# Picking expert numbers on VectorE: 16-bit pairs and lists in SBUF, and a tree of four additions in place of a reduction

## The reference

```
q = (h @ w_query).reshape(tokens, 8 heads, 256)
s1, s2 = scores of the two halves of q against 128 keys each
v1, i1 = top_k(s1, 16);  v2, i2 = top_k(s2, 16)
cand = (v1[:, None] + v2[None, :]).reshape(256)
top_s, top_c = top_k(cand, 16)
e1 = i1[top_c // 16];  e2 = i2[top_c % 16]
expert = e1 * 128 + e2
g = softmax(top_s)
act = gelu(u_tab[expert] . h);  out = sum(g * act * v_tab[expert])
```

## Time and profile before

| | us |
|---|---|
| median of 3 runs | 1533.51 |
| runs | 1533.39 to 1535.49 |
| span of the profiled execution, first to last instruction | 1527.6 |
| the profiled execution's own time | not listed; the median less the span is 5.9 |
| PE busy in the span | 1499.3 (98%) |
| DVE busy | 1196.7 (78%) |
| POOL busy | 1018.7 (67%) |
| ACT busy | 703.2 (46%) |

### The profile page before, as it was taken

The page is one execution under the profiler, slowest core; times in us unless marked ns, Lnnn a source line. Parts: engine busy times, 40 slices in busy tenths (PEclk is TensorE's granted clock), DMA queues, the critical chain, the costliest instruction groups (busy, mean ns, idle before and its releaser), DMA issues.

```text
span 1527.6 us, 21847 instructions
## 1 busy us (share of the span) xinstructions
PE 1499.3 (98%) x7983; PEld 1254.4 (82%) x7983; DVE 1196.7 (78%) x1979; ACT 703.2 (46%) x1312; POOL 1018.7 (67%) x623
## 2 busy tenths in 40 slices
PE   8999999999999999999999999999999999999997
PEld 4336684488899999999999999988888887888886
DVE  6858833526799899998888880288998898899998
ACT  2024653343344433488888883433333333333333
POOL 2602002653378888776777875698888888889866
PEclk8999999999999999999999999999999999999999
DMA  9976138033178898889999997799999999999981
GB/s 365 337 222 114 29 99 287 37 129 110 39 268 320 318 329 309 295 295 374 362 374 365 378 358 296 261 371 360 379 373 363 376 388 379 373 384 377 374 282 69
DMA packets 216600, 439.99 MB, mean 288 GB/s; under 512 B 38181, under 2 KB 128805, under 8 KB 214573
## 3 DMA queue, kind: packets, MB, share of 16 engines
q1 hardware_dynamic: 178764, 303.49, 56.7%
q0 software_dynamic: 36864, 134.23, 23.7%
q10 hardware_dynamic: 864, 0.86, 0.2%
HBM read 380.72 MB, written 56.64 MB: 286 GB/s over the span
## 4 chain that ended last, share of the span: by engine, by line
PE 71%; DMA 6%; DVE 5%; issue 4%; POOL 3%; ACT 2%; SPq 1%; DVEq 0%; ACTq 0%
PE ps L1834 12%; PE ps L1835 11%; PE ps L1836 11%; PE ps L1857 6%; PE ps L1858 6%; PE ps L1859 6%; DMA v_raw<-in_peer_v 3%; DMA a_in<-act_scr 3%; POOL vl L1725 2%; PE ps L1503 2%; PE ps L1505 2%; PE ps L1504 2%; PE ps L1849 1%; PE ps L1850 1%; PE ps L1302 1%
## 5 line engine op out<-in xcount | busy, mean ns | idle before, releaser
L1719 POOL TENSOR_TENSOR utl<-u_raw,uth 128x1024 fp32r<-128x1024 f32 x128 | 312.9, 2445 | 139.0 <-ACT uth L1738 120.7
L1834 PE MATMUL ps<-h2h,uth 128*128 128x384 f32 x1024 | 347.8, 340 | 2.2 <-POOL utl L1719 1.5
L1725 POOL TENSOR_TENSOR vl<-v_raw,vh 128x1024 fp32r<-128x1024 f32 x128 | 310.2, 2425 | 52.0 <-ACT vh L1738 50.1
L1836 PE MATMUL ps<-h2h,utl 128*128 128x384 f32 x1024 | 342.9, 335 | 0.0
L1835 PE MATMUL ps<-h2l,uth 128*128 128x384 f32 x1024 | 342.6, 335 | 0.0
L1857 PE MATMUL ps<-vh,wh 128*128 128x512 f32 x768 | 300.1, 391 | 1.8 <-DVE wl L2055 1.7
L1859 PE MATMUL ps<-vh,wl 128*128 128x512 f32 x768 | 299.3, 390 | 0.0
L1858 PE MATMUL ps<-vl,wh 128*128 128x512 f32 x768 | 299.2, 390 | 0.0
L2050 DVE TENSOR_TENSOR w_f<-a_in,g_in 128x384 f32<-128x384 f32 x128 | 206.3, 1612 | 99.7 <-DMA a_in<-act_scr 98.7
L1738 ACT ACTIVATE vh<-v_raw 128x1024 fp32r<-128x1024 f32 x128 | 135.4, 1058 | 199.2 <-DMA v_raw<-in_peer_v 167.3
L1834 PEld LDWEIGHTS ps<-h2h,uth 128*128 128x128 f32 x1024 | 192.5, 188 | 2.7 <-POOL utl L1719 1.8
(11 more groups left out here) (370 smaller groups left out, 2239.4 us busy)
## 6 DMA issues: line engine op xcount, KB each, us to landing
u_raw<-in_peer_uT SPq DMA_DIRECT2D x128, 512.0 KB, 6.5
v_raw<-in_peer_v SPq DMA_DIRECT2D x128, 512.0 KB, 9.5
act_scr<-acts SPq DMA_DIRECT2D x64, 384.0 KB, 4.6
g_scr<-stage SPq DMA_DIRECT2D x12, 2048.0 KB, 9.7
g_in<-g_scr SPq DMA_DIRECT2D x32, 768.0 KB, 9.1
a_in<-act_scr SPq DMA_DIRECT2D x64, 384.0 KB, 9.8
w_ada<-in_w_ada SPq DMA_DIRECT2D x10, 2048.0 KB, 14.9
w_q<-in_peer_w_query SPq DMA_DIRECT2D x8, 1024.0 KB, 5.8
```

What stands on the lines that cost most here:

```text
L1719: tt(k.utl[b % 3][:, :, :].rearrange(f3), k.u_raw[:, b % 4].rearrange(f3), k.uth[b % 3][:, :, :].bitcast(F32).rearrange(f3), ALU.subtract) ...
L1725: tt(k.vl[:, n % 4], k.v_raw[:, n % 4], k.vh[:, n % 4].bitcast(F32), ALU.subtract).then_inc(k.vl_done, 1)
L1834: mm(o, hi, k.h2h[:, kt, SP:T], start=(kt == 0), stop=False)
L1836: ins = mm(o, lo, k.h2h[:, kt, SP:T], start=False, stop=(kt == DK - 1))
```

## The change

Three small tiles are added in SBUF: `place_p`, `idx_h` and `iota16h`, all of 16 bits. The list 0 to 15 and the key numbers are now read from SBUF in 16 bits. Each place is written twice, as a pair, so that the comparison and the product have a stretch of at least two neighbouring 16-bit values as the innermost dimension of every operand. The sum over sixteen becomes four additions of halves. So a side has eight instructions where it had four: two copies, the comparison, the product and four additions. No DMA is added or moved, and no other engine's order changes.

```diff
+    k.place_p = k.sb("place_p", [P, PH * PTOP, 2], 91, F16)
+    k.idx_h = k.sb("idx_h", [P, PH, PTOP], 91.5, F16)
+    k.iota16h = k.sb("iota16h", [P, PTOP], 91.75, F16)
...
-                v.tensor_copy(idxf, k.idx[:, it % 2, :, side, :])
-                step(tt(e3, k.cabf[:, side].unsqueeze(2).broadcast_to([P, PH * PTOP, PTOP]),
-                        iota16.unsqueeze(1).broadcast_to([P, PH * PTOP, PTOP]), ALU.is_equal))
-                step(tt(e4, e4, idxf.unsqueeze(2).broadcast_to([P, PH, PTOP, PTOP]), ALU.mult))
-                ins = v.tensor_reduce(k.route[:, it, side], e3, AXX, ALU.add)
+                in_pairs = [P, PH * PTOP, PTOP // 2, 2]
+                v.tensor_copy(k.idx_h[:, :, :], k.idx[:, it % 2, :, side, :])
+                step(v.tensor_copy(k.place_p[:, :, :], k.cabf[:, side].unsqueeze(2).broadcast_to([P, PH * PTOP, 2])))
+                step(tt(e3.rearrange("p n (a two) -> p n a two", two=2), k.place_p[:, :, :].unsqueeze(2).broadcast_to(in_pairs),
+                        k.iota16h[:, :].rearrange("p (a two) -> p a two", two=2).unsqueeze(1).broadcast_to(in_pairs), ALU.is_equal))
+                step(tt(e4, e4, k.idx_h[:, :, :].unsqueeze(2).broadcast_to([P, PH, PTOP, PTOP]), ALU.mult))
+                for n in (8, 4, 2):
+                    step(tt(e3[:, :, 0:n], e3[:, :, 0:n], e3[:, :, n:2 * n], ALU.add))
+                ins = tt(k.route[:, it, side], e3[:, :, 0], e3[:, :, 1], ALU.add)
...
-        v.tensor_copy(iota16, k.iota16[:, :])
+        v.tensor_copy(k.iota16h[:, :], k.iota16[:, :])
```

More of the change, by code:

```diff
@@ L1906, in _ @@
         done = {"rows": 0}
-        idxf = ps[:, 5, 0:P].rearrange("p (h c) -> p h c", h=PH)
         cab = ps[:, 5, P:3 * P].bitcast(U32).rearrange("p (d c) -> p d c", d=2)
-        iota16, best, gsum = ps[:, 5, 3 * P:3 * P + PTOP], ps[:, 5, 3 * P + 16:3 * P + 24], ps[:, 5, 3 * P + 24:3 * P + 32]
+        best, gsum = ps[:, 5, 3 * P + 16:3 * P + 24], ps[:, 5, 3 * P + 24:3 * P + 32]
         first_vals = ps[:, 5, 3 * P + 32:3 * P + 64].rearrange("p (h c) -> p h c", h=2)
```

## The result

| | median of runs, us | range, us | profiled execution: time / span, us |
|---|---|---|---|
| before, 4 runs | 1533.45 | 1528.19 to 1535.49 | not listed / 1527.6 |
| after, 4 runs | 1545.22 | 1544.87 to 1549.07 | 1545.19 / 1543.3 |

The ratio of after to before is 1.0107, with a 95% interval of 1.0085 to 1.0128: slower, and by more than the 0.2% that can be told from no change. The medians lie 11.8 us apart, which alone would be a ratio of 1.0077, and the two spans 15.7. The difference lies in the base: after's profiled execution has only 1.9 us around its span (1545.19 - 1543.3), and in every run whose span is on record it is 1.75 to 1.95; so a span of 1527.6 belongs to a run of about 1529.5 and not of 1533.5.

What follows compares the result with a forecast made beforehand. PE bounds the kernel, with DVE almost as tight in the search. DVE's extra 17.5 us (sides 16.8, copy 0.7), less 7.5 row waits and 0.6 slack, delays PE 9.4: 1533.5 + 9.4 = 1543 us; own range 1537 to 1552, wider 1535 to 1561.

Steps and rivals of the forecast that it cites:

- The row that the prediction took for a copy: Evidence that SBUF-to-SBUF copies on DVE also meet POOL: 1.35 us beside POOL, 0.81 without.
- Strictly alternate: DVE and POOL, both with long strings, take turns; a waiting POOL wins the gap between two DVE steps; cycle 0.76 us.
- The rival of 2.28: Pairs do not double the rate: comparison and product stay at 2.28 us, sides 14.5 us, time 1585; chance 0.04.
- The 7.5 us of row waits: DVE's waits for gathered rows in the search, six times, expected to absorb part of DVE's 17.5 us of extra time.
- The queues that the prediction named behind the waits: Late DVE stops POOL in its first gather and a later one, and ACT at the softmax in block 48.
- I take two: S = 4.75 + 4.50 = 9.25: Each side meets two POOL subtractions, 2.25 us each, on 4.75 us of own work: 2.1 us longer than before.
- the line through 128 and 2048 values: Cost of DVE's additions: 0.29 and 2.28 us give the slope, halved for 16 bits, with 0.15 us fixed.
- 5.9 us above it, for what lies around the span, which I leave unchanged: Base of the forecast: median of runs 1533.5 us, above the profiled span of 1527.6.
- the rival of three meetings: Each side meets three POOL subtractions and lasts 11.5 us, 27 us lost, time 1561; chance 0.13.
- POOL gives way: Rival: a side meets one subtraction on average, lasts 7.0 us, routes come in time, 1533.5; chance 0.13.
- A gain: Rival: nothing meets, DVE saves 19 us, but PE can gain at most 1.5 us: 1532; chance 0.03.
- Whole holds: Shared SBUF port locked for whole instructions: 0.27 us more in each of 16 meetings, 4 us more, 1547.

Runs made afterwards that it cites:

- the experiment with the copy by way of PSUM: The kernel after, with the copy of the key numbers made in two steps through PSUM; 1547.76 us, ratio 1.0116 to the kernel before.
- the short subtraction: The kernel after, with POOL subtracting only 64 of 1024 columns in blocks 3 to 56; 1529.84 us, ratio 1.0008 to the kernel before.
- the kernel made late without meetings: The kernel before, with each side's comparison (one operand in PSUM) done twice; 1540.76 against 1529.86 us, ratio 1.0069.
- the kernel with the additions alone: The kernel before, with four additions replacing the reduction, comparison and product still reading list and key numbers from PSUM; 1532.81 against 1529.49 us, ratio 1.0019.

## Why the prediction was right, and where it was off

**The direction and the mechanism** held. Seven of the eight instructions of a side are held by POOL in one side or another of the kernel after, and the eighth, the copy of the places, in the experiment with the copy by way of PSUM; alone they are shorter (5.17 against 7.12 us), and the short subtraction takes the loss away. The row that the prediction took for a copy is a normalisation; that copies meet POOL is shown by the key numbers, 1.72 us against 0.23. "Strictly alternate" held in the main: POOL takes the gap between two steps of DVE when it is waiting. The six cases told above are its limits: there POOL went first although DVE had begun, or went twice. POOL was pushed back now and then (7 of 54 subtractions in the search over 2.5 us), which was foreseen and doesn't matter, as the kernel made late without meetings shows.

**The rate.** 1.21 us was taken for the long steps; they take 1.22 to 1.23 where they meet nothing. The rival of 2.28 is out.

**What absorbs it.** The 7.5 us of row waits are gone, and the kernel made late by a known 18.6 us lost 10.9, beside 10.5 by this step. The queues that the prediction named behind the waits are the three that show in the kernel after.

**The step that failed** is the one that reads "I take two: S = 4.75 + 4.50 = 9.25". Measured is 10.26: own work of 5.17, and 5.09 of meetings, which at 2.25 each is 2.3 of them; counted one by one they are 19 in eight sides, 2.4 a side. Both terms were too small. The own work, because the short additions don't get cheaper as the line through 128 and 2048 values says: 0.45, 0.44 and 0.43 us for 512, 256 and 128 values, where 0.42, 0.28 and 0.29 were put down. The meetings, because the formula's 2.5 was rounded down to two on the ground that POOL gives way at times. The formula itself came to 10.3. That it hit so closely is partly luck: with the measured own work and POOL's measured pace in the search (54 subtractions in 237.3 us, one in 4.39) it gives 5.17 / (1 - 2.25 / 4.39) = 10.6. Eight sides at 1.01 us more are 8.1 us on PE.

**Terms left out.** The lowered clock behind block 55 adds 0.8 us net of the wait that it hides. The `cabf` step ahead of the sides already met POOL before, and after the change it meets it less: -2.0 us. Shifting a string of work against POOL's rhythm moves all its meetings, not the new ones alone.

**The base.** "5.9 us above it, for what lies around the span, which I leave unchanged" was wrong: it is 1.9 us. The three runs shown were in the upper part of what this kernel does (1525.8 to 1536.0 in the runs beside the experiments), and the profiled execution in the middle. By the prediction's steps with measured sizes: DVE's +15.8 us less 0.6 of slack, and 0.8 for the clock, is 16.0 us, where PE shows 16.1; on 1529.5 this makes 1545.5, and measured is 1545.22. The predicted 1543 is near it by luck, because two errors offset each other: a loss of 9.4 us that should have been 16, on a base 4 us too high. The true loss lies between the forecast and the rival of three meetings (27 us).

**The rivals.** POOL gives way: no, sides are over the 8.2 us at which it decides. A gain: no, and the short subtraction shows that even without a meeting there is none to be measured. Whole holds (1547): by the prediction's own numbers a hold of 2.39 us instead of 2.25 is 0.14 more in each of 16 meetings, 2 us and not 4. Measured, the 19 holds cost 41.5 us, 2.2 each.

## What to carry to other kernels

Ask of each cheaper instruction not only what it takes alone but where its operands lie and what another engine does there: here an operand in PSUM kept a slow step clear of another engine's long reads, and the step that was twice as fast in SBUF cost more. Where one engine's string of short steps meets another's regular long instruction, price the string with S = own + hold x S / period (own: the string alone; hold: what one meeting costs; period: from one start of the long instruction to the next), keep the fraction, and look which older steps of the string shift against that rhythm too. And before saving time on an engine, look at what it waits for: in this search 2 us saved in each side only lengthened its waits, while time lost came out one to one as soon as those waits were used up.

## What the runs showed of the hardware that was not expected

- *The clock.* The granted clock fell to half, 1.2 GHz, behind waits of PE of 5.06 and 6.51 us, and not behind 0.80 us in the same trace or the 1.53 of the earlier trace rows. Windows of the kernel after, behind the waits of 0.80 and of 5.06 us:

```profile
445.00:480.00 35.00, 34.86 (x201) 34.86 (x202) 34.18 (x61) 15.05 (x20) 33.10 (x20) 1.00 0.93 319
...
500.40:503.00 2.60, 2.60 (x8) 2.60 (x9) 2.57 (x19) 0.00 (x0) 2.48 (x2) 0.50 0.95 339
```

  In the kernel made late it fell behind a wait of 4.34 us as well (0.78 on average from 652 to 658), and behind one of only 1.98 (0.50 from 623.9 to 627.2); behind the 2.41 us in the kernel with the additions alone it stayed at 1.00 (641.5 to 648). So the length of the wait alone doesn't decide, and what does is not shown here. The prediction had no term for it. Ahead of block 55 it costs nothing, since PE meets DVE there again; behind it, 0.8 us.
- *A 16-bit operand in PSUM* keeps the doubled rate: 2048 values in 1.221 us. The Trainium skill, "VectorE: DVE Perf Modes", perf-mode tier table, gives a `tensor_tensor` with any operand in PSUM the single rate; the measurement decides. It is true here of the product of the earlier trace rows, with 32-bit key numbers in PSUM (2.29 us); the comparison there also reads one value repeated, which takes the doubled rate away in SBUF as well.
- *Short strided additions* in 16 bits hardly get cheaper with size: 0.449, 0.444 and 0.428 us for 512, 256 and 128 values, where 1024 take 0.696.
- *Writes and reads are apart.* A fill on POOL holds a copy on DVE (1.43 us instead of 0.23) and not an instruction with two inputs (1.67 us for three additions, as alone).
- *Behind a gather* POOL's subtraction went ahead of a step of DVE that had begun up to 0.5 us earlier, five times in the eight sides of the kernel after; the comparison at 472.90 took 3.97 us instead of 1.22 by it.
